# Mixture-of-experts stage of a transformer block: experts from the seventh on taken in order of falling token count, their weights loaded by a list made on chip, and the last eight on 32 slots each, four side by side

## The reference

```python
def hier_moe(h, w_rg, w_re, w_e_in, w_e_out):
    t = h.reshape(-1, D)
    pg = jax.nn.softmax((t @ w_rg).astype(jnp.float32), axis=-1)
    gp, gi = lax.top_k(pg, 1)                       # one group of 4
    le = ...                                        # the 8 logits of that group
    ew, ei = lax.top_k(jax.nn.softmax(le, axis=-1), TOP_K_INNER)   # 2 of its 8 experts
    ew = ew / jnp.sum(ew, axis=-1, keepdims=True)
    weights = gp * ew
    eid = gi * EXPERTS_PER_GROUP + ei
    gates = jnp.einsum('tk,tke->et', weights, jax.nn.one_hot(eid, N_EXPERTS, dtype=jnp.float32))

    def body(acc, inp):
        wi, wo, ge = inp                            # 1024x512 and 256x1024, float32
        a, u = jnp.split(t @ wi, 2, axis=-1)
        return acc + ((jax.nn.silu(a) * u) @ wo) * ge[:, None], None

    y, _ = lax.scan(body, jnp.zeros(t.shape, jnp.float32), (w_e_in, w_e_out, gates))
```

## Time and profile before

| | us |
|---|---|
| median of 3 runs | 1130.77 (1129.78 to 1132.71) |
| the profiled execution: its own time | 1134.31 |
| its span, first to last instruction | 1132.5 |
| TensorE busy | 1084.8 (96%) |
| VectorE busy | 698.7 (62%) |
| ScalarE busy | 513.7 (45%) |
| mean granted TensorE clock | 0.985 |
| chunk 1 issued | 175.5 |
| up(0) begins | 212.7 |
| first FFN matmul begins | 458.0 |

### The profile page before, as it was taken

One profiled execution on the slowest core, in us unless ns is written; L12 is line 12 of the kernel. 1 busy time (PEld: TensorE's weight loads), 2 busy tenths in 40 slices (PEclk: granted clock), 3 DMA queues, 4 the chain that ended last, 5 costly groups with the idle time before them and its releaser, 6 DMA issues.

```text
span 1132.5 us, 18996 instructions
## 1 busy us (share of the span) xinstructions
PE 1084.8 (96%) x7922; PEld 931.8 (82%) x7922; DVE 698.7 (62%) x1129; ACT 513.7 (45%) x803; POOL 0.2 (0%) x4
## 2 busy tenths in 40 slices
PE   5989999999999999999999989899999999999997
PEld 3779888645555554899999979898899999999996
DVE  1889868323323333786865688977666775655667
ACT  3774233211111112754543468478953554443455
POOL 0000000000000000000000000000000000000000
PEclk9999999899999999999999999999999999999998
DMA  9955627999999957557355423443346545545321
GB/s 382 394 197 203 254 77 302 378 422 421 421 420 417 418 223 297 188 182 260 124 211 209 152 96 131 152 146 113 113 176 225 204 171 202 186 168 205 130 94 38
DMA packets 38153, 257.71 MB, mean 228 GB/s; under 512 B 4368, under 2 KB 5264, under 8 KB 7856
## 3 DMA queue, kind: packets, MB, share of 16 engines
q1 hardware_dynamic: 36720, 252.38, 58.0%
q10 hardware_dynamic: 1344, 4.08, 0.9%
HBM read 255.39 MB, written 1.05 MB: 226 GB/s over the span
## 4 chain that ended last, share of the span: by engine, by line
PE 64%; DVE 12%; ACT 6%; issue 3%; DVEq 0%; ACTq 0%
PE bank L537 63%; DVE wl L1817 4%; ACT wh L1248 2%; DVE xt L1867 1%; DVE rstd L1841 1%; DVE acc L1879 1%; DVE hl L1884 1%; ACT arena L1258 1%; PE bank L924 0%; ACT yl L1258 0%; DVE arena L2387 0%; ACT arena L1596 0%; ACT L1258 0%; ACT L1649 0%; PE bank L829 0%
## 5 line engine op out<-in xcount | busy, mean ns | idle before, releaser
L537 PE MATMUL bank<-hh,wh 128*128 128x256 f32 (+2 forms) x1256 | 363.4, 289 | 5.4 <-DVE wl L1817 3.1
L537 PE MATMUL bank<-hh,wl 128*128 128x256 f32 (+2 forms) x1256 | 359.3, 286 | 0.0
L537 PE MATMUL bank<-hl,wh 128*128 128x256 f32 (+2 forms) x1256 | 359.2, 286 | 0.0
L1817 DVE TENSOR_TENSOR wl<-raw,wh 128x1024 fp32r<-128x1024 f32 (+4 forms) x238 | 268.1, 1163 | 79.5 <-ACT wh L1248 76.5
L1248 ACT ACTIVATE wh<-raw 128x1024 fp32r<-128x1024 f32 (+4 forms) x238 | 227.8, 1003 | 70.0 <-PE bank L537 69.9
L537 PEld LDWEIGHTS bank<-hh,wh 128*128 128x128 f32 (+1 forms) x1256 | 241.8, 193 | 12.8 <-issue 7.1
L537 PEld LDWEIGHTS bank<-hl,wh 128*128 128x128 f32 (+1 forms) x1256 | 241.8, 193 | 1.0
L537 PEld LDWEIGHTS bank<-hh,wl 128*128 128x128 f32 (+1 forms) x1256 | 241.8, 192 | 0.9
L537 PE MATMUL bank<-yh,wh 128*128 128x256 f32 x512 | 146.7, 286 | 0.5 <-DVE yl L1837 0.5
L537 PE MATMUL bank<-yl,wh 128*128 128x256 f32 x512 | 145.4, 284 | 0.0
L537 PE MATMUL bank<-yh,wl 128*128 128x256 f32 x512 | 145.4, 284 | 0.0
(11 more groups left out here) (279 smaller groups left out, 1376.4 us busy)
## 6 DMA issues: line engine op xcount, KB each, us to landing
raw<-in_gu SPq DMA_DIRECT2D x40, 1024.0 KB, 12.8
arena<-in_gu SPq DMA_DIRECT2D x24, 1024.0 KB, 11.6
raw<-in_gd SPq DMA_DIRECT2D x22, 1024.0 KB, 10.2
raw<-in_w_adt SPq DMA_DIRECT2D x14, 1024.0 KB, 6.4
raw<-in_f1g SPq DMA_DIRECT2D x11, 1024.0 KB, 4.8
raw<-in_f1d SPq DMA_DIRECT2D x11, 1024.0 KB, 5.0
raw<-in_f2g SPq DMA_DIRECT2D x11, 1024.0 KB, 4.9
raw<-in_f2u SPq DMA_DIRECT2D x11, 1024.0 KB, 4.8
```

Of the source, the lines that this page charges most:

```text
L537: return pe.matmul(o, l, m, start=start, stop=stop, skip_group_check=True)
L1817: v.tensor_tensor(WL[slot_of[U]][:, 0:n], src, WH[slot_of[U]][:, 0:n].bitcast(f32), ALU.subtract).then_inc(S("wl"), 1)
```

## The change

Experts 0 to 5 (`FIXED` = 6) keep their places. The others are put in order of falling token count: a 32x32 comparison of keys (count times 32 plus a tie-break from the new constant `order`) gives each expert its position, `PERM` is that permutation as a matrix, and a matmul turns it into the list `ORD` of expert numbers. SP reads an entry of it (`value_load`) before the first chunk of each expert from the seventh on and takes the chunk's address from it. The gates and the one-hot matrix are put in that order by matmuls with `PERM`, and ranks are made anew. The first 24 positions are 12 blocks as before (`WIDE` = 12); the last eight are two blocks of four experts with 32 slots each. Eight experts at the end of the order never have over 32 tokens, since 512 pairs can't give 19 experts 33 each. `gather` and `scatter` run 7 times instead of 8.

```diff
+        FIXED, WIDE = 6, 12
+        BLOCKS = [(2 * g, 2) for g in range(WIDE)] + [(2 * WIDE + 4 * r, 4) for r in range(2)]
+        LAST_W = [NR + 2, NR + 5, NR, NR + 3]
...
-            if c == last_e - 11:
+            if c == last_e - 5:
                 for r in EXTRA_W:
                     ring.remove(r)
+                ring.extendleft(reversed(LAST_W))
+            if c == last_e - 1:
+                for r in LAST_W:
+                    ring.remove(r)
...
+            mm(b[0:32, 96:97], OHE3[:, 0, :], ones[:, 0:1], True, False)
+            mm(b[0:32, 96:97], OHE3[:, 1, :], ones[:, 0:1], False, True)
...
+            def order_list(name):
+                b = take(pe, name)
+                pe.wait_ge(*nth("perm", 1))
+                mm(b[0:1, 0:32], SEQC, PERM, True, True).then_inc(S("ord_mm"), 1)
...
+                        if q == 0 and x == 2:
+                            evicted(pe, "rank")
+                            order_list("ord")
...
-                            for e in range(2):
-                                c = 128 * j + 64 * e
-                                t = mm(b[64 * e:64 * e + 64, :], XG[q % 2][:, x, c:c + 64], w[e][:, k, :], x == 0, x == 7)
-                        t.then_inc(S("used"), 4)
+                            for e in range(n):
+                                c = 128 * j + cap * e
+                                t = mm(b[cap * e:cap * e + cap, :], XG[q % 2][:, x, c:c + cap], w[e][:, k, :], x == 0, x == 7)
+                        t.then_inc(S("used"), ready[u])
...
                 gather(0)
-                for p in range(16):
-                    up(p)
+                gates_turned(("srt", 0))
+                for p in range(WIDE):
+                    up(p, (4, 4), (lambda: gates_sorted(("srt", 1), ("srt", 0))) if p == 0 else None)
+                    if p == 0:
+                        ranks_sorted(("srt", 2), ("srt", 1))
                     if p > 2 and p % 2:
                         scatter(p // 2 - 1)
                     if p:
-                        down(p - 1)
+                        down(p - 1, 4)
                     turn_slots(p)
-                    if p % 2 and p < 15:
+                    if p % 2:
                         gather(p // 2 + 1)
-                down(15)
-                scatter(7)
+                down(WIDE - 1, 0)
+                up(WIDE, (4, 16))
+                scatter(WIDE // 2 - 1)
+                turn_slots(WIDE)
+                down(WIDE, 4)
+                up(WIDE + 1, (4, 16))
+                turn_slots(WIDE + 1)
+                down(WIDE + 1, 8)
+                scatter(NB // 2 - 1)
...
+            step(v.scalar_tensor_tensor(KR, bank("rank")[0:32, 64:96], 32.0, BIASR, ALU.mult, ALU.add))
+            v.scalar_tensor_tensor(KC, bank("rank")[0:32, 96:97], 32.0, BIASC, ALU.mult, ALU.add).then_inc(copied("rank"), 1)
+            chain(v.tensor_tensor(CMP, KR, KC.broadcast_to([32, 32]), ALU.is_gt))
+            chain(v.tensor_reduce(POS, CMP, AX.X, ALU.add))
+            v.tensor_tensor(PERM, SEQ32, POS.broadcast_to([32, 32]), ALU.is_equal).then_inc(S("perm"), 1)
...
+                if c in by_order:
+                    name, at = by_order[c]
+                    if not experts:
+                        sp.wait_ge(*nth("ord", 1))
+                    if at[0] not in experts:
+                        experts[at[0]] = sp.value_load(ORD[0:1, at[0]:at[0] + 1], min_val=0, max_val=31)
+                    src = D["gu"][experts[at[0]], at[1]] if name == "gu" else D["gd"][experts[at[0]]]
                 if follows[c] >= 0:
                     given_back(sp, follows[c])
```

More of the change, by code:

```diff
@@ L26 @@
 st scr o gsq gn og yo_h yo_l
-ohe rank tm tm_h flag pg g32 ghl moe
+tm tm_h pg g32 ghl moe
 g_gx g_gc g_pt g_s g_tr g_d g_yh g_sc
@@ L54 @@
     "gated_h": [("rg_h", 4), ("gain", 8)],
+    "chosen": [("ohe", 1), ("ord", 1)],
+    "ranked": [("rank", 1), ("ord_mm", 1), ("srt", 3)],
+    "decided": [("flag", 1), ("perm", 1)],
     "norm_t": [("n2_t", 8), ("hn_t", 8)],
@@ L251, in program @@
         RSXa2, RSXb2 = (v.unsqueeze(1).broadcast_to([128, 2, 256]) for v in (RSXa, RSXb))
-        chunks, where = [], {}
+        chunks, where, by_order = [], {}, {}
         def add(name, i):
@@ L256, in add @@
             where[name, i] = len(chunks)
-            chunks.append((a[i], a.shape[2], name not in ("w_ada", "w_adt", "w_r", "gu", "gd")))
+            at = {"gu": (2 * (i // 4) + i % 2, i // 2 % 2), "gd": (i,)}.get(name, (i,))
+            if name in ("gu", "gd") and at[0] >= FIXED:
+                by_order[len(chunks)] = name, at
+            src = a[at[0], at[1]] if name == "gu" else a[i]
+            chunks.append((src, a.shape[-1], name not in ("w_ada", "w_adt", "w_r", "gu", "gd")))
         def add_all(*named):
@@ L860, in raw_view, with gates_turned, gates_sorted, ranks_sorted @@
                 return RAW[raw_of[c]][:, :].rearrange("p (k n) -> p k n", k=nk)
+            def order_list(name):
+                b = take(pe, name)
+                pe.wait_ge(*nth("perm", 1))
+                mm(b[0:1, 0:32], SEQC, PERM, True, True).then_inc(S("ord_mm"), 1)
+            def gates_turned(name):
+                b = take(pe, name)
+                pe.wait_ge(*nth("g32", 1))
+                for a in range(2):
+                    t = pe.transpose(b[0:32, a * 128:a * 128 + 128], G32E[:, a, :], ident)
+                t.then_inc(S("srt"), 1)
+            def gates_sorted(name, turned_to):
+                b = take(pe, name)
+                evicted(pe, turned_to)
+                for a in range(2):
+                    t = mm(b[:, 32 * a:32 * a + 32], GT[:, a * 128:a * 128 + 128], PERM, True, True)
+                t.then_inc(S("srt"), 1)
+            def ranks_sorted(name, sorted_to):
+                b = take(pe, name)
+                evicted(pe, sorted_to)
+                mm(b[:, 0:32], TRI, OHE3[:, 0, :], True, True)
+                mm(b[:, 32:64], ones, OHE3[:, 0, :], True, False)
+                mm(b[:, 32:64], TRI, OHE3[:, 1, :], False, True).then_inc(S("srt"), 1)
             def grouped():
@@ L1026, in tensor_program @@
                 grouped()
-                evicted(pe, ("gt", 15))
+                evicted(pe, ("gt", NB - 1))
                 first_block()
@@ L1470, in highs @@
                         else:
-                            done(a, "gd", 2 * p + 1)
+                            down_done(a, p)
                         a.activation(YGH[:, j, 512 * x:512 * x + 512], bank(("gy", p, x))[:, :], ACT.Copy).then_inc(S("g_yh"), 1)
                 gathered(0)
-                for p in range(16):
-                    done(a, "gu", 4 * p + 3)
+                for p in range(NB):
+                    if p == WIDE:
+                        highs(p - 1)
+                    up_done(a, p)
                     if p >= 2:
@@ L2200, in grouped @@
                 gathered(0)
-                for p in range(16):
+                gates_turned(("srt", 0))
+                for p in range(NB):
                     q = p // 2
+                    if p == 0:
+                        gates_sorted(("srt", 1))
+                    if p == WIDE:
+                        lows(p - 1)
                     v.wait_ge(*nth("g_s", p + 1))
```

154 lines of the change are left out of this document (108 added, 46 removed).

## The result

The kernel now takes 1115.57 us (median of 4 runs, 1113.22 to 1117.22) where the kernel before takes 1131.74 beside it (4 runs, 1129.78 to 1134.09): a ratio of 0.9847 with a 95% interval of 0.9825 to 0.9869, that is 16 us less by the medians and 15 to 20 by the interval. The profiled executions differ by 1134.31 - 1115.59 = 18.7 us. Predicted were 20.0 and 1110.8, in a range of 1105 to 1121. So the sign and the range were right, and the likeliest time 4.8 us low; 1.0 of these lies in the base, since the forecast was taken off a median of 1130.77 in the table of times and the kernel before now has 1131.74.

The account below looks back on a forecast made before the run. TensorE was taken as the bound, loads just ahead. Start-up, tail loads and hand-over put the FFN at 437.7 instead of 458.03, 20.3 us; less 0.3 for constants, 20.0: 1110.8 us off the median, range 1105 to 1121.

Parts of the forecast that it names:

- The bound, and the loads ahead of it: Experts' stage before: TensorE sets the pace, asking for 408 GB/s where the DMAs reach 420, so loads run slightly ahead.
- The floor per chunk: Expert loads: at 420 GB/s the DMAs need at least 2.50 us for each chunk of 1.049 MB.
- Four places at once: Wide blocks: four 32-column matmuls run at once on TensorE, so a wide `up` takes 7.0 to 7.7 us.
- rival 1: Wide blocks: four places don't run at once, each wide `up` takes 14 us; gain 6, time 1124.6; chance 0.04.
- The anchor: Loads before the change: from bytes moved, chunk 90 has landed by about 406 us and chunk 86 by 396.
- Rival 3: Tail: no gap in the loads, chunk 96 at 421, and a costless start-up; gain 25.5, time 1105; chance 0.05.
- The chain of loads: Tail: chunk 87 issued at 399.0, landing 4.8 us later, then 9 steps of 2.50 us to chunk 96 at 426.3.
- The hand-over: Stage's end: f1g 0 lands at 428.8, ACT and DVE split it before `lows(13)`; FFN at 437.7, 20.3 us sooner.
- Copies out of PSUM: Tail: a skill rule says copies may become the bottleneck; the forecast counted only two waits of about 1 us.
- The start-up and the pairs: Before and in the first block: extra rank, ordering and gate steps cost 1.1 us, bounds 0.4 to 2.5.
- the larger constants: Kernel start: constants grow from 135 KB to 168 KB and delay TensorE's first matmul by 0.3 us.
- the long wait: Tail: TensorE's 5.0 us wait ahead of `down(13)` may drop the clock, losing 1.7 us, hidden behind DVE's f1g 0.

Follow-up runs that it names:

- the kernel without the hole: Changed kernel with the last eight experts' chunks loaded in the order TensorE reads them, buffers given back right after use: 1114.63 us, ratio 0.9840.
- the early-buffers kernel: Changed kernel with the router's small buffer at the end of the ring, so chunks 9 to 15 don't wait for it: 1116.59 us in one execution.
- the kernel with both edits: Changed kernel with the last eight experts' chunks loaded in reading order and the router's small buffer at the ring's end: 1113.24 us, ratio 0.9832.
- both kernels with the block's results ahead of f1g 0: The kernel with both edits, last block's output split before f1g 0: 1111.84 us; the same plus idle matmuls that keep TensorE's clock: 1112.82 us.

## Where the prediction was right, and where not

**The bound, and the loads ahead of it.** Right. With the tail's loads cut to a quarter the stage is 5.9 us shorter, with SP's work taken away it is the same, with the order alone it is 0.7 longer. The floor per chunk, 2.50 us, is what the traces show. The 26 reads of the list stand in after's trace (ns: least, median, most):

```profile
L2773 SPq TENSOR_LOAD <-arena x26: 263/268/469, 211.6 to 402.6; - x26
```

The Trainium skill gives about 0.6 us for a `tensor_load` ("DMA: Bandwidth & Descriptors", section "Latency and other measured facts"). The trace has 0.27, and the measurement decides: 26 of them are 7 us, not 16.

**Four places at once.** Right. The wide `up(12)` takes 7.1 us (394.95 to 402.03), in the 7.0 to 7.7 of the forecast, and rival 1 is out.

**The anchor.** "So chunk 90 has landed by about 406" was wrong: landings trail the bytes. Before, chunk 90 landed at 408.4, and 86 at 397.4. The queue was therefore not yet empty at 396: in after 86 landed at 400.4, though by 398 to 399 us the DMA share was down to 0.08. The forecast didn't feel this, since its chain starts anew with the issue of 87 (399.0 forecast, 398.79 measured) and its landing (403.8 and 403.6). Rival 3 rests on it: it gave 5.5 us more for a tail without a hole and a start-up at no cost, and the kernel without the hole gained 2.6.

**The chain of loads.** "426.3" for chunk 96 was 427.5. This is the term that was mis-sized: 9 steps of 2.50 us make 22.5, and they took 427.5 - 403.6 = 23.9, since one of them was 4.0. That a full queue lands each chunk one floor behind the last was taken as given; the traces show steps that are longer by up to 1.7 us (last section). Everything behind chunk 92 is later by it: the second half of `up(13)` at 417.69 (416.3 forecast), `down(13)` at 427.63 (426.3), the FFN at 438.80 (437.7).

**The hand-over.** Right, and it was the place where a wait took the place of another. From f1g 0's landing to the FFN's first matmul the forecast had 8.9 us, measured are 438.80 - 429.99 = 8.8. `down(13)` ran at the lower clock as forecast, and DVE's work on f1g 0 hid it. How thin that cover was the forecast didn't say. ACT had the second half of `down(13)` copied at 433.7 and DVE came to it at about 434.0, so 0.3 to 0.4 us were left. With the loads short, f1g 0 is early and the dip is worth 1.6 us; with the chunks as read 0.5 of it shows; with matmuls that keep the clock in after, TensorE waits for DVE instead and the clock falls in `scatter(6)`.

**Copies out of PSUM.** The Trainium skill ("TensorEngine Tiling (Array Packing)", PSUM Bottleneck) warns that they may become the bound once TensorE is four times faster. In the sum they were two waits of about 1 us. Measured are 1.64 us ahead of `scatter(5)`, which the sum didn't have, and 1.91 ahead of the transposes of block 13. In after they lie ahead of waits for loads and cost nothing. In the kernel with short loads 1.91 and 0.62 us stand ahead of `down(13)` and 1.64 behind it, and no DMA is waited for any more. So while the loads set the end, no trace shows the rule; with the loads out of the way, waits for copies of 1.9 and 1.6 us are what TensorE is left with in the tail. Whether the copies would bound it no run shows, since none makes them faster.

**The start-up and the pairs.** 1.1 us were forecast. Two executions with the same clock at 195 to 215 us (0.83, then 1.00) put `up(0)` at 209.34 without and 210.03 with the steps of the change, so 0.7; that is one pair of executions. Another 0.7 came inside the first block, by the kernel with the order alone, where the sum had 0.4 for `gates_sorted` and let `ranks_sorted` cost nothing. Together 1.4 in place of 1.1. (The terms as listed, 0.3 + 0.2 + 0.1 + 0.4, make 1.0; and of the last 80 chunks 78 are by the list. Neither moves the forecast by more than 0.1.) The 0.3 us for the larger constants no run can tell from the spread of the start.

**The sum.** Of the 1.1 us of start-up 0.7 lie ahead of `up(0)`, so by the stage the forecast was 437.7 - 213.4 = 224.3 us; measured are 226.1. The 1.8 us are 0.5 up to the issue of 87 (the first block, 0.3, among them), 1.4 in the chain of loads and -0.1 in the hand-over. In the time 20.0 was forecast, 18.7 is the difference of the profiled executions, and 16.2 that of the medians. What separates the last two is the spread of the executions, and no run tells it apart from a cost of the change.

## What to carry to other kernels

When TensorE and the loads are both near full, a cut on TensorE is worth only what the loads leave over. Take the landing of the last chunk, one floor per chunk back to the last time the queue was empty, and check which buffers hold up the issue there. Give short dependent work on the other engines a place ahead of long work that only prepares the next stage, and then look at what comes behind it, since two waits of 1 to 2 us in a row hide one another: each cured alone showed the next. And compare stages by their length, not by absolute times, when the start of a stage moves by several us between executions.

## What the runs showed of the hardware

**The clock near the experts' start differs between executions.** Two kernels that differ only in the order of the tail's loads show it, in the stretch before `up(0)`; the rows of the early-buffers kernel above (`up(0)` at 214.55) stand against these of the kernel with both edits (210.03):

```profile
195.00:205.00 10.00, 9.05 (x57) 7.98 (x57) 7.55 (x34) 5.50 (x11) 0.00 (x0) 0.83 1.01 419
205.00:215.00 10.00, 10.00 (x65) 6.42 (x66) 4.77 (x21) 3.07 (x4) 0.00 (x0) 1.00 1.02 423
```

A clock of 0.63 and 0.68 against 0.83 and 1.00 over the same work goes with a start that is 4.5 us later; 1.3 of them are there already when chunk 1 is issued (175.3 against 174.0).

**The clock fell after short waits.** In the kernel with short loads, 1.91 and 0.62 us of idle time with 0.41 of transposes between them were enough, behind `up(13)` with its 32-column matmuls. In after it fell behind the 1.91 and the first 0.7 us or so of the 3.97: from 420 to 425 us the mean was 0.94, from 425 on 0.50, so the fall was at about 424.4. The forecast put it down to the long wait; less was enough. A wait of 1.64 us alone ahead of a scatter didn't do it (the row at 403.67 of after, 400 to 405 at 1.00).

**Late landings come with a packet of the instruction queue.** At 420 GB/s a full queue lands a chunk every 2.5 us, but some steps are 3.4 to 4.2, while the bytes run on: from 405 to 435 us after moved 423 GB/s, and chunk 92 was 1.5 us late in it. The page's part 3 lists, beside the loads' queue q1, queues of the kind `instruction`. After's view of the DMA queues from 413 to 418 us, around that landing, has

```profile
q8 instruction: 1, 0.02, 1.3%
```

That is one packet of 16 KB, from 414.9 to 415.9 us. Over the twelve traces (chunks 11 to 96 and the FFN's first four) 27 steps between landings are over 3.3 us for a chunk that was issued more than 4 us before the landing ahead of it, and each of the 27 has such a packet between 0.6 us before that landing and its own; of the 988 other steps of this kind 123 have one. So a late landing comes with a packet, but most packets make none late, as the one at 412.8 us in the kernel with the chunks as read. Nor does it take a hole: both kernels with the block's results ahead of f1g 0 issue 87 about 3 us before 86 lands, so that the queue doesn't run empty, and have a step of 3.5 us at chunk 92. A reading that fits is that the packet holds up one of the 16 DMA engines for its 1.0 us and more, and a chunk has landed only when the last engine is through. The end of chunk 86 in after looks like that:

```profile
398.00:399.00 1.00, 1.00 (x16) 0.38 (x12) 0.00 (x0) 0.00 (x0) 0.00 (x0) 1.00 0.08 33
```

The DMA share of 0.08 is 1.3 engines of 16, 1.4 us before the chunk has landed. It is a reading of traces: no run takes the packets away.
